# Value projections turned round, normaliser states as a 129th column, and another order of VectorE's work in the mLSTM heads

## What is computed

```
layer 0:  x += 0.5 * swiglu(rmsnorm(x));  x += mLSTM mixer(rmsnorm(x));  x += 0.5 * swiglu(rmsnorm(x))
shared:   k, v = split(rmsnorm(x) @ w_kv)
layer 1:  x += 0.5 * swiglu(...);  x += block-sparse attention with ALiBi (q of its own, shared k, v);  x += 0.5 * swiglu(...)
y = rmsnorm(x)
```

```
sw   = (q k^T) * exp(d - m_loc)                       # d: decay between tokens, causal
num  = w_inter * (q C) + sw v;   qn = w_inter * (q n) + sum(sw)
h    = num / max(|qn|, exp(-m_loc))
C'   = a C + sum_s w_s k_s v_s^T;   n' = a n + sum_s w_s k_s
out  = (sigmoid(o) * rmsnorm_per_head(h) * g_head) @ w_out
```

## Time and profile before

| what | value |
| --- | --- |
| median of three runs | 1271.05 us |
| the profiled execution's own time | 1270.95 us |
| its span | 1269.2 us |
| PE busy | 1242.3 us, 98% |
| VectorE (DVE) busy | 737.7 us, 58% |
| ScalarE (ACT) busy | 582.5 us, 46% |
| GpSimd (POOL) busy | 96.2 us, 8% |
| mean DMA rate | 158 GB/s |
| granted TensorE clock, mean over the span | 0.997 |

### The profile page before, as it was taken

One profiled execution on the slowest core, in us unless ns is written; L12 is line 12 of the kernel. 1 busy time (PEld: TensorE's weight loads), 2 busy tenths in 40 slices (PEclk: granted clock), 3 DMA queues, 4 the chain that ended last, 5 costly groups with the idle time before them and its releaser, 6 DMA issues.

```text
span 1269.2 us, 22196 instructions
## 1 busy us (share of the span) xinstructions
PE 1242.3 (98%) x8929; PEld 1217.6 (96%) x8929; DVE 737.7 (58%) x1156; ACT 582.5 (46%) x918; POOL 96.2 (8%) x117
## 2 busy tenths in 40 slices
PE   6999999999999999999999999999999999999996
PEld 6999999999889999999999999999996899999996
DVE  7565655565787655554555565654556576565433
ACT  7454533443455554533334554533443465454332
POOL 3000001100323000000000000000020110000011
PEclk9999999999999999999999999999999999999998
DMA  8434244633434444334543744334567743433441
GB/s 303 166 132 165 101 137 153 206 125 124 136 123 148 160 158 139 138 114 159 179 166 133 241 147 151 136 114 144 184 232 287 282 162 133 165 133 123 137 137 41
DMA packets 35994, 200.50 MB, mean 158 GB/s; under 512 B 4362, under 2 KB 6538, under 8 KB 20450
## 3 DMA queue, kind: packets, MB, share of 16 engines
q1 hardware_dynamic: 33858, 192.34, 43.7%
q0 software_dynamic: 2080, 7.39, 1.8%
HBM read 193.14 MB, written 6.57 MB: 157 GB/s over the span
## 4 chain that ended last, share of the span: by engine, by line
PE 92%; DVE 3%; issue 1%; ACT 1%; DMA 1%; SPq 0%; POOL 0%; POOLq 0%; DVEq 0%; ACTq 0%
PE bank L429 30%; PE bank L431 30%; PE bank L430 30%; DMA raw<-vc_in 1%; DVE cn L1495 0%; PE bank L539 0%; ACT junk L1059 0%; DMA raw<-w_in 0%; PE bank L550 0%; DVE dmat L1450 0%; PE bank L489 0%; DVE x L1729 0%; PE bank L761 0%; ACT dmat L1052 0%; DVE w_lo L1244 0%
## 5 line engine op out<-in xcount | busy, mean ns | idle before, releaser
L429 PE MATMUL bank<-h_hi,w_hi 128*128 128x320 f32 x1920 | 597.5, 311 | 11.5 <-DVE h_lo L1256 10.5
L431 PE MATMUL bank<-h_hi,w_lo 128*128 128x320 f32 x1920 | 594.1, 309 | 0.0
L430 PE MATMUL bank<-h_lo,w_hi 128*128 128x320 f32 x1920 | 594.1, 309 | 0.0
L919 ACT ACTIVATE w_hi<-raw 128x1024 fp32r<-128x1024 f32 (+1 forms) x368 | 335.8, 959 | 458.4 <-PE bank L431 454.2
L1244 DVE TENSOR_TENSOR w_lo<-raw,w_hi 128x1024 fp32r<-128x1024 f32 (+1 forms) x368 | 392.9, 1109 | 117.9 <-ACT w_hi L919 117.8
L429 PEld LDWEIGHTS bank<-h_hi,w_hi 128*128 128x128 f32 x1920 | 361.2, 188 | 14.1 <-DVE w_lo L1244 10.4
L430 PEld LDWEIGHTS bank<-h_lo,w_hi 128*128 128x128 f32 x1920 | 361.3, 188 | 0.4
L431 PEld LDWEIGHTS bank<-h_hi,w_lo 128*128 128x128 f32 x1920 | 361.2, 188 | 0.0
L430 PE MATMUL bank<-f_lo,w_hi 128*128 128x320 f32 x704 | 216.5, 308 | 0.0
L429 PE MATMUL bank<-f_hi,w_hi 128*128 128x320 f32 x704 | 216.5, 307 | 0.0
L431 PE MATMUL bank<-f_hi,w_lo 128*128 128x320 f32 x704 | 216.5, 307 | 0.0
(11 more groups left out here) (208 smaller groups left out, 616.5 us busy)
## 6 DMA issues: line engine op xcount, KB each, us to landing
raw<-w_in SPq DMA_DIRECT2D x88, 1024.0 KB, 4.8
raw<-w_out SPq DMA_DIRECT2D x64, 704.0 KB, 4.1
raw<-w_a SPq DMA_DIRECT2D x12, 1024.0 KB, 4.8
raw<-w_kv SPq DMA_DIRECT2D x8, 1024.0 KB, 4.8
raw<-vc_in SPq DMA_DIRECT2D x16, 512.0 KB, 6.4
raw<-kc_in SPq DMA_DIRECT2D x12, 512.0 KB, 4.7
raw<-w_oa SPq DMA_DIRECT2D x4, 1024.0 KB, 5.2
raw<-w_q SPq DMA_DIRECT2D x4, 1024.0 KB, 4.8
```

What stands on the lines that cost most here:

```text
L429: pe.matmul(out, wh, mh, start=first, stop=False)
L430: pe.matmul(out, wh, ml, start=False, stop=False)
L431: return pe.matmul(out, wl, mh, start=False, stop=last)
L919: sc.activation(w_hi[:, n_at % 2, part * w:part * w + w], raw[:, raw_of(n_at) % RAW, part * w:part * w + w], ACT.Copy).then_inc(hi_done, 1)
```

## The change

Three things are changed.

1. **Value projections.** The tokens become the stationary operand and 512 value features the moving one, so that the product comes out token-major. A pair of units (4 contraction tiles of 512 features each) fills three banks: two blocks of 128 prompt tokens with three passes, and one for the samples, whose hi and lo parts stand side by side in `hs` (64 + 64 columns) and need two passes. Per unit these are 32 matmuls of 512 columns. ScalarE gathers `hs`, and the RMSNorm factor, which is now one number per partition, comes from `token_totals` (matmuls with one column) as `rcol`. ScalarE evacuates the prompt's banks, ScalarE and VectorE together the samples'. `turn_values` and the scaling into `v_st` are gone.
2. **Normaliser states.** The matmuls of the states take all 129 columns of `v_tok`, so n is the 129th column of C; `cn`, `cpn` and the outputs are one column wider. The separate matmuls and VectorE steps are gone. The prompt states are multiplied in 32-column tiles instead of 64-column tiles.
3. **Heads.** VectorE no longer does `gate_half` (the factor 1/2 goes into the gain, and `gated` adds 1), nor the steps of `denominators`: ScalarE squares the denominator, and the squared lower bound `least` is made once for all heads. `spread_keys` moves from GpSimd to VectorE, the copy of the prompt state from VectorE to ScalarE. `decay(h+1)` and `spread_queries(h+1)` stand first in an iteration; on ScalarE the exponentials, in three pieces of which one reads PSUM directly, stand ahead of `head_squares(h)`. `spread_maxima(h+2)` stands behind `o_chunk(h+1)`. `head_turn(7)` stands before the sixth tile of the output projection.

The room of `work` shrinks, so the second early key unit lies in `row_room` and in the room of the norm; SP loads its second page after the fourth layer norm's reciprocal.

```diff
-state_part = [bank[7][:, 0:128], bank[7][:, 128:256], bank[2][:, 256:384], bank[2][:, 384:512]]
+state_part = [b[:, at:at + DV + 1] for b, at in ((bank[7], 0), (bank[7], 129), (bank[2], 129), (bank[2], 258))]
+            def token_totals():
+                for t in range(2):
+                    pe.matmul(bank[6][:, 320 + t:321 + t], sqsum[:, 128 * t:128 * t + 128], ones[:, 0:1],
+                              start=True, stop=True)
+                for g in range(2):
+                    pe.matmul(bank[6][64 * g:64 * g + 64, 322:323], sqsum[:, TP:T], ones[:, 0:1],
+                              start=True, stop=True, skip_group_check=True)
+            def value_tile(s, kt, t, out):
+                w = (kt % 4) * 512
+                wh, wl = w_hi[:, s, w:w + 512], w_lo[:, s, w:w + 512]
+                first, last = kt == 0, kt == KT - 1
+                if t < 2:
+                    tok = slice(128 * t, 128 * t + 128)
+                    pe.matmul(out, h_hi[:, kt, tok], wh, start=first, stop=False)
+                    pe.matmul(out, h_lo[:, kt, tok], wh, start=False, stop=False)
+                    return pe.matmul(out, h_hi[:, kt, tok], wl, start=False, stop=last)
+                pe.matmul(out, hs[:, kt, :], wh, start=first, stop=False)
+                return pe.matmul(out, hs[:, kt, :], wl, start=False, stop=last)
...
-            units(U_A, P_A, 1, 4)
-            turn_values(P_A + 2, 0)
...
+            value_unit(U_A + 2, 0, V_BANKS[0])
+            value_unit(U_A + 3, 1, V_BANKS[0])
+            pe.wait_ge(pair_free, P_A + 1)
+            value_unit(U_A + 4, 0, V_BANKS[1], sample_wait=lambda: pe.wait_ge(v_kept, 1))
+            value_unit(U_A + 5, 1, V_BANKS[1])
...
             o_chunk(0)
+            spread_maxima(1)
             for h in range(H):
                 head_outputs(h)
-                if h + 1 < H:
-                    spread_maxima(h + 1)
                 sample_states(h)
                 if h + 1 < H:
                     if h % 2:
                         scores_of_two(h + 1)
                     o_chunk(h + 1)
-                else:
-                    pe.wait_ge(p_done, H)
-                    for t in range(2):
-                        pe.matmul(bank[4][0:1, :], ones[:, 0:1], kw[:, t, :], start=(t == 0), stop=(t == 1))
...
+                    if h + 2 < H:
+                        spread_maxima(h + 2)
                 if h + 1 < H:
                     head_turn(h)
...
-                if kt == 2:
+                if kt == 5:
                     head_turn(H - 1)
...
             def decay(h):                                   # ScalarE
                 sc.wait_ge(d_done, h + 1)
-                sc.activation(dmat[:, :], dmat[:, :], ACT.Exp).then_inc(w_done, 1)
+                sc.wait_ge(qm_done, 2 * h + 2)
+                sc.activation(dmat[:, 128:256], bank[4][:, 128:256], ACT.Exp, bias=cols[:, 0, h:h + 1]).then_inc(w_done, 1)
+                for part in (slice(0, 128), slice(256, 448)):
+                    sc.activation(dmat[:, part], dmat[:, part], ACT.Exp).then_inc(w_done, 1)
...
             for h in range(H):                              # ScalarE
-                head_squares(h)
                 if h + 1 < H:
                     decay(h + 1)
-                    head_scale(h)
...
+                head_squares(h)
+                if h % 2 == 0:
+                    prompt_state(h)
...
+                head_scale(h)
...
             for h in range(H):                              # VectorE
-                denominators(h)
-                variances(h)
                 if h + 1 < H:
                     decay(h + 1)
                     spread_queries(h + 1)
+                else:
+                    z_split(0)
+                    z_split(1)
+                ve.wait_ge(head_o, h + 1)
+                if h + 1 < H:
+                    spread_keys(h + 1)
+                if h % 2 == 0:
                     weights(h + 1)
-                    states(h)
+                variances(h)
+                if h % 2 and h + 1 < H:
+                    weights(h + 1)
...
+                states(h)
+                if h + 1 < H:
                     for k, part in HALVES.get(h, ()):
                         split_half(U_A + k, U_A + k, part)
                     keep_gate(h + 1)
                     gated(h)
-                    gate_half(h + 1)
...
+            load_early(0, 0)                                # SP
+            load_early(0, 1)
+            load_early(1, 0)
+            load_cache(EARLY)
+            sp.wait_ge(rms_done, 5)
+            load_early(1, 1)
```

More of the change, by code:

```diff
@@ L525, in ffn @@
                         out_chunk(i * 2 + j, j, False)
-            groups = [0]
-            def turn_values(p, v_unit):
-                pe.wait_ge(pair_free, p + 1)
-                for c in range(2):
-                    g = groups[0]
-                    groups[0] += 1
-                    if g >= 2:
-                        pe.wait_ge(tr_free, g - 1)
-                    for t in range(3):
-                        w = 128 if t < 2 else NS
-                        mm = pe.transpose(bank[4 + g % 2][0:w, t * 128:t * 128 + 128],
-                                          v_st[:, v_unit % 2, c, t * 128:t * 128 + w], ident)
-                    mm.then_inc(tr_done, 1)
+            def token_totals():
[5 more added lines that the diff above has]
+                              start=True, stop=True, skip_group_check=True)
@@ L653, in head_outputs @@
                     for t in range(2):
-                        for g in range(2):
-                            pe.matmul(bank[2][64 * g:64 * g + 64, 0:DV], kw[:, t, (h + g) * 64:(h + g) * 64 + 64],
-                                      v_tok[:, t, h + g, 0:DV], start=(t == 0), stop=(t == 1),
+                        for a in range(4):
+                            pe.matmul(bank[2][32 * a:32 * a + 32, 0:DV + 1], kw[:, t, h * 64 + 32 * a:h * 64 + 32 * a + 32],
+                                      v_tok[:, t, h + a // 2, :], start=(t == 0), stop=(t == 1),
                                       skip_group_check=True)
@@ L1534, in _ @@
                     gated(h)
-                    gate_half(h + 1)
                 else:
-                    z_split(0)
-                    z_split(1)
-                    states(h)
-                    for g in range(2, H - 1):
+                    for g in range(4, H - 1):
                         z_split(g)
@@ L1859, in _plain_units, with _value_units @@
     return _pair_units(w, [256 * u for u in range(n)], [256 * u + 128 for u in range(n)])
+def _value_units(w):
+    import numpy as np
+    a = w.reshape(2, 4, 128, 2, 512)
+    return np.ascontiguousarray(a.transpose(3, 0, 2, 1, 4)).reshape(4, 128, PAIR)
 def kernel(**inputs):
```

376 lines of the change are left out of this document (209 added, 167 removed).

## The result

The changed kernel takes 1273.57 us (median, 1272.6 to 1274.8), the kernel before beside it 1271.47: ratio 1.0016, 95% interval 1.0009 to 1.0022. It is 2 us slower, where I had forecast 1.1 us faster. The profiled executions say the same: 1272.9 us against 1270.95, the granted clock 0.997 in both.

The account below looks back on a forecast made before the run. It took PE's instruction stream as the clock, with an equally long loop of other engines in the heads. Terms -5.2 - 1.7 + 1.7 + 4.1 = -1.1 took 1270.95 to 1269.8 us; eight in ten, 1264.3 to 1275.0.

Parts of the forecast that it names:

- transposes and value matmuls: Value projections: eight `turn_values` calls vanish, -5.2 us; 256 matmuls of 512 columns replace 384 of 320, -1.7 us.
- token totals: Ahead of the square totals: 16 new one-column passes on PE at 0.108 us, +1.7 us (0 to 2.4).
- normaliser sums, end of head 7: Output projection: nearly 3 us of removed PE work become waits for the next weights, 0 us (-2 to +0.5).
- the rest: Other edits, such as the 129th column and the later early key page: zero, up to +1 us.
- a floor that vanishes under longer matmuls: Value units: the surplus over 2.4 GHz at 320 columns disappears at 512, giving 213.3 ns a matmul, -1.7 us.
- a fixed charge: Value units, a bound: each matmul pays the same surplus at any width, 226.5 ns at 512 columns, +1.7 us.
- Heads beside PE: Heads: a VectorE, ScalarE and GpSimd loop lengthens to 8.3 us and makes PE wait, net +4.1 us (+2.5 to +5.6).
- PE's own need: Heads: PE's work without waits falls to 7.03 us a head, saving 1.3 us over seven heads.
- the ring: Heads: VectorE, ScalarE and GpSimd steps from one head's squares to the next, 7.21 us before, 8.3 after (7.9 to 8.6).
- A: Heads: the loop beside PE has unseen room, heads -1.3 us instead of +4.1, total 1264.4 us; chance 0.23.
- B: Value units: 512-column matmuls cost by width, 234.4 ns, total 1275.3 us; milder form, fixed charge, 1273.3; chance 0.17 together.
- C: Value stage: PE waits for a bank or the gathered samples, 1273.8 us; chance 0.10 together with a longer loop.

Follow-up runs that it names:

- experiment 3: Changed kernel with each 512-column matmul of the value units split in two of 256 columns: 1276.48 us.
- experiment 2: Changed kernel with ScalarE's squares again ahead of the next head's exponentials and VectorE's variances ahead of the weights: 1266.89 us, ratio 0.9963.
- 6: Kernel before with only the heads' and normalisers' parts, squares ahead of exponentials, value projections and transposes kept: 1269.00 us, ratio 0.9980.
- 8: Changed kernel with only ScalarE's squares put back ahead of the exponentials, VectorE's order kept: 1269.75 us, ratio 0.9986.
- 9: Kernel before with only the heads' and normalisers' parts, in the changed kernel's order, value projections and transposes kept: 1275.31 us, ratio 1.0031.
- 10: Changed kernel with only VectorE's variances put ahead of the weights for even heads too, ScalarE's order kept: 1273.79 us, ratio 1.0019.
- experiment 1: Kernel before with the value projections of the change alone, including new places of its buffers and early key pages: 1271.42 us, ratio 0.9995.
- experiment 4: Changed kernel with the three passes of a prompt value tile reordered so h_hi is stationary twice in a row: 1273.78 us.

## Why the prediction was wrong, step by step

The ledger, by PE's starts in the two profiled executions:

| step | forecast | measured |
| --- | --- | --- |
| transposes and value matmuls | -5.2 - 1.7 = -6.9 | -3.3 (2 x -1.66) |
| token totals | +1.7 | +1.3 (2 x 0.64) |
| heads, with the first `spread_maxima` ahead of them | +4.1 | +3.1 (2.94 + 0.19) |
| normaliser sums, end of head 7 | 0 | +0.6 |
| the rest | 0 | +0.3 |
| sum | -1.1 | +2.0 |

**Value projections: the step that failed.** The prediction took "512 columns at 213.3 ns", a floor that vanishes under longer matmuls. They take 226.9, and experiment 3 shows a fixed 13 ns on each matmul in the floor's place: 256 x 226.9 = 58.1 us against 56.3, +1.8 instead of -1.7. This 3.5 us error is larger than the whole distance between forecast and result (3.1), and it alone turned the sign. The prediction had the right number among its bounds ("a fixed charge gives 226.5 ns, +1.7") and with it named 1273.3 us, close to what came; in part that is luck, as the heads came 1.0 us and the token totals 0.4 below their forecasts while other stages came 0.9 above. It preferred the floor because two longer kinds of matmul showed no surplus, the 267 ns steps of the start and the two passes of the total. Both readings hold within what two starts resolve; the inference did not. They differ from a fast pass at full clock in more than length (one runs at the lower level of the clock by its steps, which fall from 267 to 147 ns for the same matmul at 15.1 to 15.3 us; the other takes two cycles a column), so they said nothing on how the surplus scales with width. The nearest rows were the 320-column steps themselves, and for them a charge is as good a reading as a floor. A longer row of the second kind stands in the trace of the kernel before, the gate matmuls, the second and the last start of 16 passes of 320 columns at two cycles each (the first row merges 15 of them):

```profile
252.67 4.20 PE L550 MATMUL bank<-x,wg 128*40 128x320 f32 x15
...
256.44 0.43 PE L550 MATMUL bank<-x,wg 128*40 128x320 f32 x1
```

3.77 / 14 = 269.3 ns a step, where 640 cycles take 266.7. So this kind has a charge too, of 2.6 ns, at a length where a floor of 147 ns would have vanished. Its surplus is a small one of its own and tells nothing of that of the fast matmuls. The changed kernel held a second witness: `spread_maxima`, 384 columns, also of the fast kind (its row has one pass, though it stands outside `passes`), takes 329.72 - 329.55 = 0.17 us, about the 160 + 13 ns of the charge.

The Trainium skill ("TensorE: Matmul & The Clock Gate", section "Back-to-back issue gap") has this form, width over 2.4 plus a constant, for a matmul by itself, and was right in direction: it said the wider form is dearer. Its constant of 2.5 ns is not that of these matmuls; the steps of 120.0, 146.5 and 226.9 ns give 13. It is near the 2.6 ns of the gate matmuls. The section gives the constant for the full clock alone and N/1.2 for the lower one, and the 267 ns steps of the start agree: their missing surplus was no sign against a charge. My sentence that the surplus is something "the wider form can shed" fell: the edit has 128 charges less, 1.7 us, but 256 x 512 columns are 8192 more than 384 x 320, 3.4 us at 2.4 GHz. The two differ by the +1.7 of the fixed charge's bound.

**Transposes, -5.2**: held. -3.3 less the +1.8 of the matmuls leaves -5.1.

**Heads beside PE, +4.1**: the mechanism held, and the waits had the forecast size: they cost 53.46 - 48.18 = 5.3 us against experiment 2, for 5.4. What was mis-sized is PE's own need, which fell by more than the forecast 1.3: with the first `spread_maxima` counted in, from 50.52 to 48.18 + 0.19 us, 2.2. Beside `spread_maxima`, the prompt states and the product ahead of them take 0.15 us less in each even head (0.92 us before, 0.77 in experiment 2). The squares stand 8.19, 8.03, 8.19, 8.04 and 8.18 us apart from head 1 on, 8.13 on average, for a forecast of 8.3. The largest miss in the ring is from squares to power, 1.37 for 1.60: the denominator's square and the second small step cost less than I added. Experiments 2, 6, 8, 9 and 10 show the order as the cause: it alone makes 53.46 us out of 48.18, with or without the value part, and the part that binds is ScalarE's, where the squares stand behind the exponentials and with them behind VectorE's decay and queries.

The prediction's picture of the loop before was too favourable, though. It took the 7.21 us between the squares of heads 3 and 4 for the loop, "as long as PE's own head". That pair is one of the short ones: the squares of heads 1 to 6 stand 7.43, 7.76, 7.21, 7.76 and 7.21 us apart in that trace, 7.48 on average, for 7.22 of PE. So the squares were already falling behind PE, by 0.26 us a head, and the loop ended before that reached a wait.

**Token totals, +1.7**: 1.3, within the bounds. The four passes that load 128 columns take 252.08 - 251.65 = 0.43 us, near the forecast 0.108 each; the four that load 64 take 0.21, half of it, where the forecast charged them in full.

**Normaliser sums, 0**: their PE work did turn into waits as forecast, 1.68 and 0.58 us for `h_lo` and 1.60 for `w_lo`, where the kernel before had 1.01 in all. 0.6 us more than that was lost, just over the bound of +0.5: `gated(7)` came at 379.41, 9.7 us after the start of head 7 and not 9.1.

**Rivals.** A (the loop has room) is refuted. B came in its milder form. C (waits in the value stage) did not: no idle time stands between the 128 matmuls. The late sample states of experiment 1 were on nobody's list. In the changed kernel they are not late: its GpSimd issues them at 336.96 us, 2.0 us ahead of the weight load of 339.00, and they land in 3.5 us. It is not the slower heads that hide them, as in experiment 2, with faster heads, no such wait appears either.

The remaining +0.3 us lie in the attention stage and before the mixer. Over the ten experiments the attention stage varied from -0.3 to +1.2 us against the kernel before, with no edit to what PE computes in it, so they are not attributed.

## What to carry to other kernels

When a step's surplus can be a floor or a charge, only a row of the same kind of instruction at another width decides; rows that differ in clock or in cycles per column do not, as here they carry surpluses of 0 and 2.6 ns and not 13. Look for the ring of engines that repeats once per iteration and ask of every moved step whether it now lies in it: 11 us less work on VectorE did not make the kernel shorter, while the order that puts decay, queries and exponentials ahead of the squares cost 5.3 us over seven heads (with VectorE's order of `weights` and variances). Measure such a ring over several iterations, since one pair may be a short one. And when a stage is made faster, see which transfer had only just been early enough.

## What the runs showed of the hardware

- A matmul of `passes` at full clock takes its columns at 2.4 GHz plus 13 ns: 120.0 ns at 256 columns, 146.5 at 320, 226.9 at 512. The charge stays when the stationary operand is the same twice in a row (experiment 4). It is absent from the 267 ns steps of the program's start, where the clock is at its lower level by these steps, and only 2.6 ns in the fp32 passes that take two cycles a column (269.3 ns at 320 columns, the clock recorded at full); what makes it was not found.
- fp32 passes of one column took 107 ns with 128 stationary columns to load and 53 ns with 64 (0.43 and 0.21 us for four each).
- A 258 KB load took 3.6 us to land in the median of experiment 1's eight. Issued 0.3 us behind a 1 MB load of another queue it took 6.9 and 7.1 there, and 5.9 and 5.8 in the kernel before.
- Two reorderings worth 0 and 3.8 us alone were worth 6.7 together. In a ring only the longer of two branches counts: in even heads of the changed kernel VectorE's `weights` end (350.60 us) before ScalarE's squares do and the variance's first step can start (350.74), so VectorE's branch became the longer one only after ScalarE's had been shortened.
